# A chunked delta rule's triangular inverse: its first levels on the array's diagonal quarters, with the transposed inverse updated instead of turned

## What is computed

```
def gated_delta_rule_chunked(q, k, v, g, beta):
    ...
    gdiff = g[..., :, None] - g[..., None, :]
    decay = jnp.where(incl, jnp.exp(jnp.where(incl, gdiff, 0.0)), 0.0)
    k_beta = k * beta[..., None]
    a_mat = jnp.where(strict, jnp.einsum('bhnid,bhnjd->bhnij', k_beta, k) * decay, 0.0)
    t_mat = a_mat + jnp.eye(GDN_CHUNK, dtype=jnp.float32)
    ...
    sol = lax.linalg.triangular_solve(t_mat, rhs, left_side=True, lower=True,
                                      unit_diagonal=True)
    u, w = sol[..., :dv], sol[..., dv:]
    qk = jnp.where(incl, jnp.einsum('bhnid,bhnjd->bhnij', q, k) * decay, 0.0)
    ...
    def step(state, inp):
        qk_c, qd_c, kd_c, u_c, w_c, gl_c = inp
        v_new = u_c - jnp.einsum('bhcd,bhde->bhce', w_c, state)
        o_c = (jnp.einsum('bhcd,bhde->bhce', qd_c, state)
               + jnp.einsum('bhij,bhje->bhie', qk_c, v_new))
        state = state * gl_c[..., None, None] + jnp.einsum('bhcd,bhce->bhde', kd_c, v_new)
        return state, o_c
    ...
o_fwd = gated_delta_rule_chunked(qg, kg, vg, g_f, beta_f)
o_bwd = flip(gated_delta_rule_chunked(flip(qg), flip(kg), flip(vg), flip(g_b), flip(beta_b)))
```

## Time and profile before

| | us |
|---|---|
| median of the runs | 2659.4 |
| lowest, highest | 2659.29, 2661.61 |
| the profiled execution, its own time | 2661.32 |
| its span | 2659.4 |
| TensorE busy in the span | 2405.9 (90%) |
| VectorE, ScalarE, GpSimd busy | 851.5, 606.1, 213.9 |
| mean granted TensorE clock | 0.972 of full speed |

### The profile page before, as it was taken

One profiled execution on the slowest core, in us unless ns is written; L12 is line 12 of the kernel. 1 busy time (PEld: TensorE's weight loads), 2 busy tenths in 40 slices (PEclk: granted clock), 3 DMA queues, 4 the chain that ended last, 5 costly groups with the idle time before them and its releaser, 6 DMA issues. The chain is left out here.

```text
span 2659.4 us, 26174 instructions
## 1 busy us (share of the span) xinstructions
PE 2405.9 (90%) x10644; PEld 1277.6 (48%) x10644; DVE 851.5 (32%) x1422; ACT 606.1 (23%) x1023; POOL 213.9 (8%) x166
## 2 busy tenths in 40 slices
PE   6999999899999999996998989898898976999878
PEld 3445554377778876443433433333333323575343
DVE  1215766534544442113110101111010104454582
ACT  2004656633333332201000000000000002223131
POOL 0000000033433331000000000000000000120000
PEclk9999999899999999998999999999999998999889
DMA  5201000010000002521799999999999991211001
GB/s 210 73 32 66 33 32 0 0 40 25 25 25 25 25 25 95 199 103 63 326 429 428 428 427 429 426 428 429 426 428 428 428 422 40 99 49 68 32 32 48
DMA packets 93386, 488.27 MB, mean 184 GB/s; under 512 B 10781, under 2 KB 37683, under 8 KB 68563
## 3 DMA queue, kind: packets, MB, share of 16 engines
q1 hardware_dynamic: 91920, 486.38, 45.0%
q10 hardware_dynamic: 1347, 0.22, 0.0%
HBM read 483.18 MB, written 3.41 MB: 183 GB/s over the span
## 5 line engine op out<-in xcount | busy, mean ns | idle before, releaser
L1364 PE MATMUL PS<-SL,R 128*64 128x512 f32 x1168 | 261.0, 595 | 38.8 <-DMA SL<-w_up 20.1
L1364 PE MATMUL PS<-R 128*64 128x512 f32 x880 | 197.2, 596 | 28.9 <-DMA R<-w_up 15.8
L1364 PEld LDWEIGHTS PS<-SL,R 128*64 128x64 f32 x1168 | 80.9, 137 | 214.0 <-issue 145.6
L1816 PE MATMUL PS<-HT,SL 128*128 128x512 f32 x384 | 169.4, 597 | 1.7 <-PEq L1559 1.7
L1005 ACT ACTIVATE SL<-PS 128x512 f32<-128x512 f32 x208 | 124.2, 597 | 122.0 <-PE PS L912 97.7
L1532 DVE TENSOR_TENSOR HT<-HT,PS 128x512 f32<-128x512 f32 x32 | 20.6, 684 | 370.5 <-PE PS L1364 370.5
L1364 PEld LDWEIGHTS PS<-R 128*64 128x64 f32 x880 | 61.1, 137 | 159.7 <-issue 108.7
L1384 PE MATMUL PS<-SL,HT 128*64 128x512 f32 x280 | 124.4, 594 | 14.8 <-ACT HT L1472 7.0
L1385 PE MATMUL PS<-SL,HT 128*64 128x512 f32 x280 | 124.9, 596 | 0.0
L625 PE MATMUL PS<-HT,SL 128*128 128x512 f32 x256 | 117.2, 612 | 0.8 <-PEq L415 0.8
L343 PE MATMUL PS<-HT,SL 128*128 128x512 f32 x256 | 114.3, 601 | 3.3 <-PEq L230 2.4
(11 more groups left out here) (365 smaller groups left out, 3687.0 us busy)
## 6 DMA issues: line engine op xcount, KB each, us to landing
SL<-w_up SPq DMA_DIRECT2D x38, 2048.0 KB, 28.0
SL<-w_gate SPq DMA_DIRECT2D x35, 2048.0 KB, 30.2
SL<-w_down SPq DMA_DIRECT2D x35, 2048.0 KB, 27.3
R<-w_gate SPq DMA_DIRECT2D x29, 2048.0 KB, 30.2
R<-w_down SPq DMA_DIRECT2D x29, 2048.0 KB, 27.3
R<-w_up SPq DMA_DIRECT2D x26, 2048.0 KB, 29.0
SL<-w_in SPq DMA_DIRECT2D x19, 2048.0 KB, 8.9
X<-w_in SPq DMA_DIRECT2D x16, 512.0 KB, 3.9
```

Source lines behind the costliest of these rows:

```text
L1364: m = pe.matmul(banks[n][half * CAP:(half + 1) * CAP, :], XC[x // 2 % 2][:, 2 * j + k, toks], w[:, k, (2 * half + n) * 512:(2 * half + n + ...
L1816: m = pe.matmul(bank_[:, :], slab(i % 2)[:, k, j * P:(j + 1) * P], hT[:, k, :], start=(k == 0), stop=(k == KD - 1))
```

## The change

1. Levels 1 to 5 work on the diagonal 64x64 blocks alone. A direction's four heads are held packed in 128x256 (64 columns a head): the upper half of the partitions holds the upper diagonal blocks, the lower half the lower ones (`packed`). Each product is two 64x64 matmuls per head, one on the quarter of the array with rows 0-63 and columns 0-63, one on rows and columns 64-127 (`for r in BLK`). The masks in the table are packed likewise.
2. X is no longer transposed at each level. XT is kept beside X (in the other 256 columns) and updated by a product of its own, `level_XT`, and a subtraction of its own on VectorE. It starts from the transposed A.
3. The two directions are shifted: the products of a level go P of d = 0, the XT product of d = 1 from the level before, P of d = 1, X of d = 0, XT of d = 0, X of d = 1.
4. The widest level alternates the directions matmul by matmul (`widest_P`, `widest_X`), each direction on another off-diagonal quarter.
5. The gates' rows are transposed from G (`rows`, one record each) instead of multiplied (two records). `gram_k` and `gram_q` of turn n+1 move in between the products of the widest level of turn n; those of turn 0 stand ahead of the first turn.
6. The extras stay whole and where they were in the order, in other banks; the second and third now wait for AT to be copied out. ScalarE copies AT in three pieces per direction. VectorE and GpSimd take the two directions' steps in other orders.
7. The last state update of each head group (`scan_s` after the last chunk), which nothing reads, is left out.
8. GpSimd clears four 64x256 pieces at the start of the stage, beside the state.

The diff, cut to what is spoken of:

```
+                def rows(n):
+                    for q, d, c, heads, B, W in each(n):
                         if n:
                             pe.wait_ge(E4["XL_ready"], q - 1)
                         for i, h in enumerate(heads):
-                            pe.matmul(part(bank(d, 1), i), gk[:, h, cs], gk[:, h, cs], start=True, stop=True)
+                            col = c * 16 + d * 8 + h
+                            m = pe.transpose(part(bank(d, 0), i), G[:, col:col + 1].to_broadcast([P, P]), ident)
+                        m.then_inc(E4["row_done"], 1)
...
                 def more(n, i):
...
-                    if n < len(PAIRS):
-                        if i < 2:
-                            pe.wait_ge(E4["dec_ready"], 2 * n + i + 1)
...
+                    elif i == 0:
+                        pe.wait_ge(E4["dec_ready"], 2 * n + 1)
+                    else:
+                        pe.wait_ge(E4["AT_ready"], 2 * n + i)
...
-                def turn_X(n, l, q, d, B):
-                    pe.wait_ge(E4["X_ready"], (n * (NL - 1) + l) * 2 + d + 1)
...
-                        m = pe.transpose(part(bank(d, 2), i), B["X"][:, i, :], ident)
-                    m.then_inc(E4["T_done"], 1)
...
+                def level_P(n, l, d_):
                     for q, d, c, heads, B, W in each(n):
-                            for i in range(4):
-                                m = pe.matmul(part(bank(d, 0), i), B["A"][:, i, :], B["X"][:, i, :], start=True, stop=True)
+                        if d == d_:
...
+                            for i in range(4):
+                                for r in BLK:
+                                    m = pe.matmul(bank(d, 0)[r, 64 * i:64 * i + 64], packed(B["A"])[r, i, :], packed(B["X"])[r, i, :],
+                                                  start=True, stop=True)
+                            m.then_inc(E4["P_done"], 1)
...
+                def level_XT(n, l, d_):
...
+                                for r in BLK:
+                                    m = pe.matmul(bank(d, 2)[r, 64 * i:64 * i + 64], packed(B["PM"])[r, i, :], packed(B["X"], 256)[r, i, :],
+                                                  start=True, stop=True)
+                            m.then_inc(E4["T_done"], 1)
...
-                    if scan:
+                    if scan and goes_on(n - 1):
                         scan_s(n - 1)
                     if inv:
-                        for l in range(1, NL):
-                            level_P(n, l)
-                            level_X(n, l)
+                        for l in range(1, NL - 1):
+                            level_P(n, l, 0)
+                            if l > 1:
+                                level_XT(n, l - 1, 1)
+                            level_P(n, l, 1)
+                            level_X(n, l, 0)
+                            level_XT(n, l, 0)
+                            level_X(n, l, 1)
+                        level_XT(n, NL - 2, 1)
+                        if n + 1 < len(PAIRS):
+                            gram_k(n + 1, 0)
+                        widest_P(n)
+                        if n + 1 < len(PAIRS):
+                            gram_k(n + 1, 1)
+                            gram_q(n + 1)
+                        widest_X(n)
...
                 def level(n, l):
...
-                            v(tt(B["X"], B["X"], f4(bank(d, 1)[:, :]), ALU.subtract), E4["X_ready"])
+                            v(tt(packed(B["X"]), packed(B["X"]), f4(bank(d, 0)[:, 256:512]), ALU.subtract), E4["X_ready"])
+                            dve.wait_ge(E4["T_done"], (n * (NL - 2) + l - 1) * 2 + d + 1)
+                            xt, dt = packed(B["X"], 256), f4(bank(d, 2)[:, 0:256])
+                            if l < NL - 2:
+                                v(tt(xt, xt, dt, ALU.subtract), E4["XT_ready"])
+                            else:
+                                for b, r in enumerate(BLK):
+                                    v(tt(W["XT"][r, :, r], xt[r], dt[r], ALU.subtract), E4["XT_ready"] if b else None)
```

More of the change, by code:

```diff
@@ new lines, in widest_P @@
+                def widest_P(n):
+                    pe.wait_ge(E4["X_ready"], (n + 1) * (NL - 1) * 2)
+                    for i in range(4):
+                        for q, d, c, heads, B, W in each(n):
+                            r, w = side(d, False), side(d, True)
+                            m = pe.matmul(bank(d, 0)[w, 64 * i:64 * i + 64], packed(B["AT"], 256)[r, i, :], packed(B["X"])[r, i, :],
+                                          start=True, stop=True)
+                            if i == 3:
+                                m.then_inc(E4["P_done"], 1)
@@ L938, in level_X, with widest_X @@
+                def widest_X(n):
+                    pe.wait_ge(E4["P_ready"], (n + 1) * (NL - 1) * 2)
+                    pe.wait_ge(E4["XT_ready"], (n + 1) * (NL - 1) * 2)
+                    for i in range(4):
+                        for q, d, c, heads, B, W in each(n):
                             r, w = side(d, False), side(d, True)
-                            for i in range(4):
-                                m = pe.matmul(bank(d, 1)[r, 64 * i:64 * i + 64], flat(B["PM"])[w, 64 * i:64 * i + 64], W["XT"][w, i, w],
-                                              start=True, stop=True)
@@ L974, in scan_s @@
                         m.then_inc(E4["s_done"], 1)
+                for d in range(2):
+                    gram_k(0, d)
+                gram_q(0)
                 for n in range(len(PAIRS) + 1):
@@ L1055, in _ @@
                 tt = nc.gpsimd.tensor_tensor
-                g(nc.gpsimd.memset(St, 0.0), E4["st_zero"])
+                g(nc.gpsimd.memset(St, 0.0))
+                for d in range(2):
+                    for b in range(2):
+                        g(nc.gpsimd.memset(bufs[d]["XT" + str(b)][BLK[1 - d], :, BLK[d]], 0.0), E4["st_zero"] if d and b else None)
                 for n in range(len(PAIRS) + 1):
@@ L1118, in _ @@
                     if scan:
[L1119 to L1123 removed]
+                        right(n - 1, 0)
                     if inv:
@@ L1131, in _ @@
                     more(n, 0)
+                    more(n, 1)
                     if scan:
[L1133 to L1140 removed]
@@ L1141, in _ @@
-                    more(n, 1)
-                    more(n, 2)
-                    if scan:
-                        for q, d, c, heads, B, W in each(n - 1):
-                            dve.wait_ge(E4["s_done"], q + 1)
-                            for i, h in enumerate(heads):
-                                col = c * 16 + d * 8 + h
-                                v(nc.vector.scalar_tensor_tensor(St[:, d * 8 + h, :], St[:, d * 8 + h, :], gl[:, col:col + 1],
-                                                                 part(bank(d, 3), i), ALU.mult, ALU.add),
-                                  E4["S_ready"] if i == 3 else None)
+                        outputs(n - 1)
@@ L1151, in _ @@
+                    more(n, 2)
+                    if scan and goes_on(n - 1):
+                        states(n - 1)
                     if inv:
```

195 lines of the change are left out of this document (120 added, 75 removed).

## The result

| | before | after |
|---|---|---|
| median, us | 2660.51 (2659.29 to 2663.67, 4 runs) | 2567.97 (2563.43 to 2571.77, 4 runs) |
| ratio | | 0.9647, interval 0.9632 to 0.9662 |
| the stage, from its block's first clearing to the next stage's first matmul, us | 520.34 | 427.41 |

The account below looks back on a forecast made before the run. TensorE was taken as the bound, busy 420.3 of 424.0 us in turns 1 to 7. Terms -74.9, -7.2, -3.75 and -2.75 sum to -88.6 us: 2661.3 to 2572.7, median 1.9 lower, 2571 us; range 2558 to 2630.

Parts of the forecast that it names:

- The group of eight small products, 0.46 us: Levels 1 to 5: 16 records on two diagonal quarters run side by side in 0.46 us; 0.93 if in turns.
- The level, 2.88 us: Each of levels 1 to 5: six groups of 0.46 us on TensorE plus late handovers, 2.88 us.
- two late handovers of 0.05: In each level, one late start of TensorE behind VectorE per direction, 0.05 us each, added to 2.8 us.
- The rest of a turn: Work after the levels; with the levels 21.7 us instead of 32.4, so 10.7 us won in each of seven turns.
- The cover at the transposition of A: Head of a turn: 9.5 us of TensorE work still covers the chain due at 8.2, with 1.3 us to spare.
- The head of turn 0, -1.35 us: Start of turn 0 up to its levels: 2.65 us less, with 1.3 us added for four more clearings.
- k and q products and rows 4.4: Head of turn 0: these TensorE products take 4.4 us, within 5.8 us to the first extra.
- Turn 7 and turn 8: Stage's end: without the last state updates and with shorter tails, -3.75 us in turn 7, -2.75 in turn 8.
- own range: Whole kernel, forecast's own case without rivals: 2562 to 2588 us, from 40 levels of 2.78 to 3.2 us.
- Side by side in part: Rival for levels and widest level: a pair takes 0.081 us, a group 0.65, +50 us, 2621 us; chance 0.17.
- In turns: Rival: the two quarters take turns, a group 0.93 us, a level 5.6, whole 2690; chance 0.12 shared with the clock.
- The clock: Rival: half the array at work lowers the clock to 1.2 GHz, levels 5.6 us; chance 0.12 shared with quarters taking turns.

Follow-up runs that it names:

- the copy for VectorE: Changed kernel plus one useless 128x64 VectorE copy ahead of direction 1's subtraction of X in levels 1 to 5: 2573.49 us.
- one quarter alone: Changed kernel with every record of levels 1 to 5 on the first quarter, same number of records, lower blocks not computed: 2674.43 us.
- the early start: Changed kernel with TensorE's wait for GpSimd's clearings moved from the stage's start to the first product that reads the states, turn 1: 2563.82 us.
- both edits: Changed kernel with direction 1's q product behind the widest X and the wait for GpSimd's clearings moved to turn 1: 2558.68 us.

## Why the prediction was right, and where it was off

**The group of eight small products, 0.46 us: right.** Measured 0.47, and 0.93 on one quarter. The rows that carried it were the two ways of halving, and the diagonal pair behaved as both together. By the Trainium skill, TensorEngine Tiling (Array Packing), Restrictions and Gotchas, different row tiles cannot access the same PSUM bank at the same time. The trace does not agree for these pairs: the two quarters write different partitions of one bank, and their records start 6 ns apart, a pair every 0.058 us. Whether two row tiles that write the same partitions of a bank would take turns was not tried.

**The level, 2.88 us: 0.08 too long.** Its main part, six groups on TensorE, was right. The two late handovers of 0.05 that I added do not exist: VectorE is 0.13 us early, and late only in the second level of turns 3 and 5. The statement behind them, that TensorE stays the bound but barely, is what the copy for VectorE showed. From the start of the levels to the k products the forecast had 15.12 us, the trace has 14.65.

**The rest of a turn.** The wait for VectorE ahead of the rows was forecast as about 0.85 and is 0.57; from the first record of the widest X to the rows it is 1.26 us, forecast 1.42. The k and q products took 1.09 and 2.87, forecast 0.98 and 2.72; the rows 0.95, forecast 0.88. These pieces come to 21.4 us, forecast 21.7. A turn won 11.4 us and not 10.7: 0.3 is this, and the other 0.4 is on the side of before, whose same work I had added up as 32.4 us and which the turn lengths put at 32.8. The cover at the transposition of A held: no idle time stands ahead of L933 in turns 1 to 7, as forecast.

**The head of turn 0, -1.35 us: wrong, +1.2.** The step that failed is "k and q products and rows 4.4". The timeline of TensorE after:

```profile
538.83 3.78 PE L892 MATMUL PS<-R 128*128 128x128 f32 x16 [4.43 <-POOL SL L1130]
542.40 2.62 PE L900 MATMUL PS<-R 128*128 128x128 f32 x16
544.86 1.04 PE L882 MATMUL PS<-tab,small 128*128 128x128 f32 x8
546.96 7.11 PE L919 MATMUL PS<-R,X 128*128 128x512 f32 x16 [1.07 <-ACT SL L1100]
```

The first 16 records take 3.57 us, 0.22 each, twice the 0.11 of the same form at full clock; from the k products to the rows it is 6.03 us, where 32 records at 0.11 are 3.5. That is 2.5 us on a term of 4.4. By stretch, the granted clock is:

```profile
520.00:530.00 10.00, 7.89 (x20) 3.23 (x18) 3.46 (x5) 5.90 (x8) 0.00 (x0) 1.00 0.00 0
530.10:538.83 8.73, 1.94 (x9) 1.57 (x9) 1.73 (x4) 4.78 (x7) 3.03 (x5) 0.50 0.25 73
538.83:543.80 4.97, 4.97 (x23) 4.97 (x24) 0.00 (x0) 0.00 (x0) 0.00 (x0) 0.50 0.34 86
```

TensorE is at its lower level, 1.2 GHz instead of 2.4, from 530.10 on. So it is not the wait for the clearings that brought the clock down: it was low before that wait began at 534.40. The fall stands in a wait of the stage before, 4.57 us ahead of L654, which ends at 532.45. The kernel before has the same fall, in a stretch that I had not looked at by itself:

```profile
534.35:539.00 4.65, 4.65 (x26) 4.65 (x27) 0.00 (x0) 0.00 (x0) 0.00 (x0) 0.61 0.75 206
```

My window ran from 534.35 to 565.82 as one row, and its mean clock hid this: I priced the new records at full clock and took them from a time of before that held the low one. In the kernel before the clock is back 3.55 us after the first product, with the change 4.97. The terms as written also add up to 6.2 us to the first extra and not to 5.8; it took 8.1. The clearings were right (1.40 us for four, forecast 1.3), and so was the wait for AT (1.20, forecast about 1.4).

**Turn 7 and turn 8: right in sign, 1.75 and 0.3 us too small.** In turn 7 the largest part is the widest level. From the end of the last XT product to the recurrence it took 2.95 us, where the forecast's terms leave 3.7: they keep 0.85 for the wait for VectorE ahead of the rows, and turn 8 has no rows. Another 0.5 is in the levels and 0.4 on the side of before, as in every turn. The states, by their undoing, give 5.2 to 5.4 us, where 1.75 + 2.75 = 4.5 were counted; the excess is the wait of 0.5 in turn 7 and 0.3 in turn 8.

**The sum.** The 2571 us came 3 us from the median, but in part by luck: the turns and the ends had been put 6.9 us too small, the head 2.6 us too well. The own range was wider than its reason, too: levels of 2.78 to 3.2 us, 40 of them, would give 2567 to 2584 and not 2562 to 2588.

**The rivals.** Side by side in part: no sign of it; two loads and two products per 0.058 us were sustained through a level. In turns: shown by experiment to give 2674 (with the widest level left in pairs), had it happened. The clock: 1.00 in all turns of the change, but not out of reach, since it fell once in two of the experiments.

## What to carry to other kernels

Products of 64x64 on the two diagonal quarters of the array cost half when they alternate. Here the two wrote one PSUM bank, on different partitions; nothing else was tried. Price such a pair by one quarter's pitch, and write the quarters alternately (26 us here).

Once TensorE's part of a loop has shrunk to the length of the chain beside it, every further move must be checked at both ends of the work that it moves: `scan_ks` hid one wait on each side, and moving it forward lost more than it won.

When a stage begins behind an idle stretch, read its granted clock in stretches of a few us. A mean over the head of a turn hid records at twice their assumed cost. Look also where the low stretch begins: here it was in the stage before, ahead of the wait that one would blame.

Compare experiments turn by turn before a difference of the whole stage is put down to an edit. In two of them here 1.6 us came from a clock that fell in one turn.

## What the hardware showed that I had not expected

TensorE started records of different quarters out of the order in which they were written. With the quarters one after the other, a group took 0.575 us and not 0.93, and records of L949 started before earlier ones of L960. The starts are the trace's; the ends of matmuls are modelled, so in what order they ended is not shown. The Trainium skill, TensorE: Matmul & The Clock Gate, Part 3: Packing small matmuls, says that matmuls are strictly in order in start and end and that only weight loads are pulled ahead; for the starts this trace does not agree. So for records on different quarters the order written, which I had called the schedule, is not strictly the order in which they start.

Where the clock comes back at the head of the stage varies with code that is the same: counted from the first product, 2.9 us (half of the q products behind the widest X) to 6.2 us (one quarter alone). With the early start it was 4.9 (5.9 with both edits), so the first 16 products still took 3.76 us. What the stretch before would have to hold for the clock to stay up was not tried.

The clock can fall inside the turns as well. With the k and q products behind both widest products, every turn holds the waits of 0.57 and 0.93 us, and in one of eight, turn 5, the 16 records behind them took 3.61 us at a mean granted clock of 0.57. With the VectorE copy the same came at the start of turn 8 (0.59), behind waits of 0.80 and 0.93. In the other turns, and in turn 7 of the change with waits of 0.56 and 0.93, it did not. What decides is open.
